# A fp32 transformer on one core: filter tiles and norm of the convolution mixer moved beside its attention, and a turned attention with values stationary in column tiles

## The reference

```python
def even_mixer(h, w_in, w_out, conv_w, conv_b, ln_g, ln_b, q_g, k_g, sinks):
    proj = h @ w_in
    a_val, a_gate, q, k, v = jnp.split(proj, cuts, axis=-1)
    u = a_val * jax.nn.sigmoid(a_gate)
    u = lax.conv_general_dilated(u, ...) + conv_b          # 31 taps, 512 channels
    u = jax.nn.silu(layer_norm(u, ln_g, ln_b))
    ...
    o, _, _ = banded_attention(q, k, v, SWA_WINDOW - 1, sinks)
    return jnp.concatenate([u, o.reshape(b, s, -1)], axis=-1) @ w_out

def causal_block_attention(q, k, v, scale):                # mla; dsa has the same with a mask from its index
    ...
        s = jnp.einsum('bqhd,bkhd->bhqk', qb, k).astype(jnp.float32) * scale
        s = jnp.where(key_pos[None, :] <= qpos[:, None], s, NEG)
        p = jax.nn.softmax(s, axis=-1).astype(v.dtype)
        return jnp.einsum('bhqk,bkhd->bqhd', p, v)
```

## Time and profile before

| | |
|---|---|
| median of three runs | 1776.69 us |
| the profiled execution | 1778.19 us |
| its span | 1776.4 us |
| mean granted TensorE clock | 0.997 |
| PE busy | 1757.5 us (99%), 9850 records |
| PEld busy | 1493.8 us (84%) |
| DVE busy | 1238.5 us (70%) |
| ACT busy | 934.9 us (53%) |
| POOL busy | 30.5 us (2%) |
| DMA | 312.06 MB, mean 176 GB/s |

### The profile page before, as it was taken

The page is one execution under the profiler, slowest core; times in us unless marked ns, Lnnn a source line. Parts: engine busy times, 40 slices in busy tenths (PEclk is TensorE's granted clock), DMA queues, the critical chain, the costliest instruction groups (busy, mean ns, idle before and its releaser), DMA issues.

```text
span 1776.4 us, 25138 instructions
## 1 busy us (share of the span) xinstructions
PE 1757.5 (99%) x9850; PEld 1493.8 (84%) x9850; DVE 1238.5 (70%) x1861; ACT 934.9 (53%) x1304; POOL 30.5 (2%) x41
## 2 busy tenths in 40 slices
PE   9999999999999999999999999999999999999998
PEld 8888878888888888888888788888888878888887
DVE  7776645876577657677656967777756778668774
ACT  6554545554455546555545545455544644555553
POOL 0000100000000001000000000000000000000000
PEclk9999999999999999999999999999999999999999
DMA  8656643666666656366656644556665554466663
GB/s 273 196 179 202 180 138 119 190 178 208 178 195 184 195 172 189 108 199 187 194 180 176 181 131 131 178 179 189 191 193 171 145 166 131 148 192 189 188 194 109
DMA packets 231294, 312.06 MB, mean 176 GB/s; under 512 B 23614, under 2 KB 179934, under 8 KB 231178
## 3 DMA queue, kind: packets, MB, share of 16 engines
q1 hardware_dynamic: 231014, 310.16, 57.7%
q10 hardware_dynamic: 164, 0.30, 0.0%
HBM read 308.71 MB, written 1.64 MB: 175 GB/s over the span
## 4 chain that ended last, share of the span: by engine, by line
PE 94%; DVE 4%; ACT 1%; issue 1%; DMA 0%; SPq 0%; POOL 0%; POOLq 0%; ACTq 0%
PE ps L657 26%; PE ps L606 16%; PE ps L608 16%; PE ps L607 16%; PE ps L659 13%; DVE wlo L1733 1%; PE ps L618 1%; PE ps L839 1%; PE ps L865 1%; PE ps L852 1%; PE ps L807 1%; ACT whi L1249 0%; DVE m_scr L1742 0%; PE ps L1151 0%; PE ps L902 0%
## 5 line engine op out<-in xcount | busy, mean ns | idle before, releaser
L1733 DVE TENSOR_TENSOR wlo<-staging,whi 128x1024 fp32r<-128x1024 f32 (+1 forms) x580 | 692.7, 1211 | 345.4 <-ACT whi L1249 344.9
L1249 ACT ACTIVATE whi<-staging 128x1024 fp32r<-128x1024 f32 (+1 forms) x580 | 606.5, 1050 | 489.8 <-PE ps L608 306.5
L657 PE MATMUL ps<-hT,whi 128*128 128x512 f32 x1984 | 623.6, 396 | 0.3 <-DVE wlo L1733 0.3
L659 PEld LDWEIGHTS ps<-hT,wlo 128*128 128x128 f32 x1984 | 372.7, 188 | 88.1
L659 PE MATMUL ps<-hT,wlo 128*128 128x256 f32 x1984 | 390.0, 278 | 0.0
L657 PEld LDWEIGHTS ps<-hT,whi 128*128 128x128 f32 x1984 | 302.1, 189 | 0.6 <-DVE wlo L1733 0.5
L606 PE MATMUL ps<-whi,fh 128*128 128x512 f32 x504 | 196.1, 389 | 0.0
L607 PE MATMUL ps<-wlo,fh 128*128 128x512 f32 x504 | 196.1, 389 | 0.0
L608 PE MATMUL ps<-whi,fl 128*128 128x512 f32 x504 | 196.1, 389 | 0.0
L606 PE MATMUL ps<-whi,hT 128*128 128x512 f32 (+3 forms) x464 | 184.2, 397 | 0.0
L608 PE MATMUL ps<-whi,hT 128*128 128x512 f32 (+3 forms) x464 | 177.4, 382 | 0.0
(11 more groups left out here) (345 smaller groups left out, 1829.9 us busy)
## 6 DMA issues: line engine op xcount, KB each, us to landing
staging<-in_w_in SPq DMA_DIRECT2D x92, 512.0 KB, 3.6
staging<-in_ffn_w_gate SPq DMA_DIRECT2D x84, 512.0 KB, 4.5
staging<-in_ffn_w_up SPq DMA_DIRECT2D x84, 512.0 KB, 4.5
staging<-in_ffn_w_down SPq DMA_DIRECT2D x84, 512.0 KB, 4.1
staging<-in_w_ffn_gate SPq DMA_DIRECT2D x44, 512.0 KB, 4.3
staging<-in_w_ffn_up SPq DMA_DIRECT2D x44, 512.0 KB, 4.6
staging<-in_w_ffn_down SPq DMA_DIRECT2D x44, 512.0 KB, 4.1
staging<-in_od_w_in SPq DMA_DIRECT2D x16, 512.0 KB, 3.7
```

Of the source, the lines that this page charges most:

```text
L657: e.matmul(o, wh[:, kk, j * 128:j * 128 + 128], hT[:, k, :], start=k == 0, stop=False)
L659: m = e.matmul(o[:, 0:256], wl[:, kk, j * 128:j * 128 + 128], hTh[:, k, :], start=False, stop=k == KD - 1)
L1249: e.activation(high(u)[:, 0:n], stage[u % NS][:, 0:n], ACT.Copy).then_inc(*K.inc("hi", ("hi", u)))
L1733: e.tensor_tensor(low_of(u)[:, 0:n], stage[u % NS][:, 0:n], high(u)[:, 0:n].bitcast(F32), ALU.subtract).then_inc(*K.inc("lo", ("lo", u)))
```

## The change

Two parts. In the even mixer the second half of the filter (`conv(2)`) becomes a generator of its own that starts in round 19 and stands behind `swa` in a round; it was a part of `products`, ahead of `swa`. The norm's mean moves from round 21 to 22, its variance from 23 to 25, and its broadcast from 25 to 27. The multiplication by the norm, Silu, and the high and low parts are made in two halves, and each row of the output product waits for its own half. The output product's `down` starts in round 23 as before.

In the four-branch mixers both attentions become `attend_turned`. Groups go by head pair: tile 0 and tile 1 of heads 0-1, then of heads 2-3. The probabilities are normalised before they are transposed: DVE takes the reciprocals of a group's sums (128x2) and ACT multiplies, two "light" copies. In the values matmuls v is stationary (128x64, in column tiles at output partitions 0 and 64) and the transposed probabilities move (128 columns), so that the output is already turned. The output scaling, the four transposes of outputs per attention and their wide copies go; ACT takes the high part (256 columns per head pair) from PSUM and DVE the low part a turn later.

```diff
@@ tensor program
+            def attend_turned(a):
+                groups = [(t, h0) for h0 in range(0, H, 2) for t in range(2)]
+                for turn in range(H + 3):
+                    sums = [turn - 3] if 0 <= turn - 3 < H else []
+                    for i in sums:
+                        t, h0 = groups[i]
+                        if t == 0:
+                            ops[h0] = room((P + " o", h0))
+                        e.wait_ge(*K.at(P + " pt", i))
+                        for kt in range(t + 1):
+                            for j in range(2):
+                                o = (j * (t + 1) + kt) * 128
+                                w = e.matmul(ops[h0][64 * j:64 * j + 64, 128 * t:128 * t + 128], a.vN(kt, h0 + j),
+                                             a.pt[i % 2][:, o:o + 128], start=kt == 0, stop=kt == t)
...
+                        e.wait_ge(*K.at(P + " light", i))
...
-                weave([(1, products()), (21, layer_norm()), (7, swa()), (23, down(g, m.rows))])
+                weave([(1, products()), (7, swa()), (19, conv(2)), (22, layer_norm()), (23, down(g, m.rows))])
...
-                    yield from attend(m.dat)
-                    yield
-                    transposed(P + "dsa", N(0, 256), 2)
+                    yield from attend_turned(m.dat)
@@ scalar program, in a turn after the exponentials
+                    if 0 <= turn - 3 < H and groups[turn - 3][0]:
+                        k = groups[turn - 3][1] // 2
+                        hi, _, at = a.dst
+                        e.wait_ge(*K.at(P + " pv", turn - 3))
+                        e.activation(hi[:, at + k, :], bk(P + " o", 2 * k)[:, 0:256], ACT.Copy).then_inc(
+                            *K.inc("oT", (P + " oT hi", k)))
+                    if 0 <= turn - 1 < H:
...
+                        e.wait_ge(*K.at(P + " one by", i))
+                        for j in range(2):
+                            e.activation(a.sm[i % 3][:, j, 0:nk], a.sm[i % 3][:, j, 0:nk], ACT.Copy,
+                                         scale=a.mx[:, 3, c0 + j:c0 + j + 1]).then_inc(
+                                *K.inc("light", *([(P + " light", i)] if j else [])))
@@ vector program
+                for turn in range(H + 3):
+                    if 0 <= turn - 4 and groups[turn - 4][0]:
+                        low(turn - 4)
+                    if 0 <= turn - 1 < H:
...
+                        e.wait_ge(*K.at(P + " ex", i))
+                        e.reciprocal(r, l).then_inc(*K.inc("att_sum", (P + " one by", i)))
+                    if turn < H:
...
+                            e.tensor_tensor_reduce(out=a.sm[i % 3][:, j, 0:nk], in0=ps[j][:, 0:nk],
+                                                   in1=a.mask(t), scale=scale(t, h0 + j),
...
-                weave([(1, products()), (18, conv()), (21, layer_norm()), (7, swa()), (23, down(g, m.rows, 1.0))],
+                weave([(1, products()), (18, conv()), (7, swa()), (22, layer_norm()), (23, down(g, m.rows, 1.0))],
```

More of the change, by code:

```diff
@@ L452, in __init__ @@
                              for k in range(4)]
-                self.rows += [(self.mh[:, k, :], self.ml[:, k, :], ("ev ml",)) for k in range(4)]
+                self.rows += [(self.mh[:, k, :], self.ml[:, k, :], ("ev ml", k // 2)) for k in range(4)]
         class Odd:
@@ L892, in products, with conv @@
                             done("ev u", j0 + j)
+                    yield from conv(0)
+                def conv(j0):
+                    ps = room(("ev tap", j0))
                     e.wait_ge(*K.at("ev w4"))
[L894 to L906, removed]
-                                yield
-                        done("ev tap", j0)
+                    for n in range(2 * STEPS):
+                        j, k = j0 + n // STEPS, n % STEPS
+                        if k == 0:
+                            e.wait_ge(*K.at("ev u4", j))
+                        c = 256 * (n // STEPS)
+                        for q in range(GROUPS):
+                            w = e.matmul(ps[32 * q:32 * q + 32, c:c + 256], m.w4[:, q, j, k, :],
+                                         m.u4[:, j, q, 4 * k:4 * k + S], start=k == 0, stop=k == STEPS - 1)
+                        if n + 1 == 2 * STEPS:
+                            w.then_inc(*K.inc("tap_mm", ("ev tap mm", j0)))
+                            done("ev tap", j0)
+                        if n + 1 in (6, 11, 16):
+                            yield
                 def swa():
@@ L1452, in swa @@
                     transposed("swa", 4, m.mh[:, 4:8, :])
-                weave([(1, products()), (6, swa()), (23, down(m.rows)), (21, layer_norm())], catch_up)
+                weave([(1, products()), (6, swa()), (22, layer_norm()), (23, down(m.rows))], catch_up)
             def odd(m):
@@ L1680, in mla @@
                     yield
[L1681 to L1683 removed]
+                    yield from attend_turned(m.mat)
                 def highs():
@@ L2390, in dsa @@
                     e.wait_ge(*K.now("dsa"))
-                    yield from attend(m.dat)
-                    yield
-                    transposed(P + "dsa", 2, m.bh[:, 4:6, :], m.bl[:, 4:6, :], (P, "branch", 2))
+                    yield from attend_turned(m.dat)
                 def gla():
@@ L2568, in mla @@
                         yield
-                    yield from attend(m.mat)
-                    yield
-                    transposed(P + "mla", 2, m.bh[:, 0:2, :], m.bl[:, 0:2, :], (P, "branch", 0))
+                    yield from attend_turned(m.mat)
                 weave([(1, gates()), (30, short_conv()), (1, dsa()), (5, gla()), (27, mla()), (TURN[0], turn()),
```

143 lines of the change are left out of this document (116 added, 27 removed).

## The result

Twenty runs of the changed kernel took 1782.85 us in the median (1778.08 to 1785.83), twenty of the kernel before, on the same chips, 1776.18 (1773.92 to 1780.03). The ratio on record is 1.0027, with a 95% interval of 1.0021 to 1.0034 (the two medians alone give 1.0038). The change made the kernel slower, by more than the forecast's bound of 0.2%, where no measurable change was forecast (1775.4). The time is above the stated range (1770.8 to 1780.0), and close to the rival B (1781.4), to which I had given 0.11.

The account below looks back on a forecast made before the run. TensorE bounds the kernel, busy 1757.5 of 1776.4 us. From 1778.19, less 2.2 (even mixer's order) and 3.0 (its clock), plus 2.4 (four-branch mixers), came 1775.4 us, range 1770.8 to 1780.0: no measurable change.

Parts of the forecast that it names:

- rival B: Four-branch mixers: the clock falls behind PE's 2.5 us idle, price 3.0 in each block, 1781.4 us; chance 0.11.
- even mixer, order and clock: Even mixer: 2.2 us gained by reordering PE's work and 3.0 by the clock no longer falling.
- wait (a): dsa, level matmuls: DVE's last score reduction starts late behind a reciprocal, PE's wait 1.1 to 2.5 us, +1.4 per block.
- wait (b): dsa, later level matmuls: PE waits for the outputs' PSUM bank until DVE's low part has read it, +1.4 per block.
- work of two attentions: Four-branch mixers, PE work: output transposes removed and values matmuls changed, 0.8 us less per attention.
- clock in the mixers: Four-branch mixers: no fall of the granted clock counted in the sum, 0 us; a fall was left to rival B.
- 1.86 idle was harmless before taps: Argument against rival B: PE's 1.86 us idle ahead of the even mixer's taps brought no fall of the clock.
- 0.75 us of new waits: Even mixer: some 0.3 us at the second turn's transposes and some 0.45 at the mean, taken as 0.75 together.
- "nothing" for the norm in two halves: Even mixer, output products: PE does not wait for normalised rows in either order, so no gain, unless late (about 0.5).
- the 0.63 taken: Four-branch mixers, values matmuls in column tiles: a block of eight was to take 0.63 us, against 0.84 before.
- the rule: Values matmuls: "Mode switching requires drain", quoted against the change; no size given, as taps run without a visible gap.
- upper bound of +7: Four-branch mixers, both blocks together: +7 us at the worst of new waits and PE work, where +2.4 was taken.

Follow-up runs that it names:

- both edits: Changed kernel with DVE's reciprocal behind the next scores' reduction and its low part of the outputs a turn earlier, ahead of the weight remainder: 1771.46 us, 0.9965 of before.
- norm late: Kernel before with only the norm a round later (mean in round 22, variance in 25, broadcast in 27), taps unmoved: 1781.14 us, 1.0017 of before.
- probes: Even mixer's part of the change, old attention, plus unused DVE additions ahead of dsa's last score reduction: three gave 1.0021, one 0.9999 of the kernel before.
- even part alone: Kernel before with only the even mixer's part of the change, attention of the four-branch mixers as before: 1773.58 us, 0.9971 of before.
- order of the tiles: Kernel with both edits, but the values matmuls run all of one head, then all of the other: 1771.56 us, 0.9967 of the kernel before.

## Why the prediction was wrong

The two profiled executions, term by term:

| term of the sum | forecast | measured |
|---|---|---|
| even mixer, order and clock | -5.2 | -4.95 |
| wait (a), per block | +1.4 | +1.37 |
| wait (b), per block | +1.4 | +1.74 and +1.59 |
| work of two attentions, per block | -1.6 | -1.24 and -1.00 (the mixers with both edits, where neither new wait stands) |
| clock in the mixers, both | 0 | about +6 |

**The step that failed** is "Against it: 1.86 idle was harmless before taps", with which I put the mixers' clock at nothing in the sum and gave rival B 0.11. I had the mechanism and its place, the wait of 2.5 us at L1201. In its place the runs showed 6.2 us of the clock in the profiled execution, as worked out below. One execution had one wait of 1.86 us with no fall behind it and one of 1.17 with a fall, and I read from these that it depends on what PE runs afterwards. The kernel with the turned attention alone showed a fall at the very same taps, with 2.27 us of idle time, so the taps are no protection; and one execution without a fall could not show that a wait is harmless, as the kernel with the norm late had none there with 2.73. The probes showed one behind 1.67 and 2.86 us with the old attention, in all of their profiled blocks, while the kernel with both edits, where PE idles 1.1 us at that place, has a mean clock of 0.998 to 1.000 in all five runs. What stood in the profile for it was plain: the change took the idle time at the level matmuls from 1.1 to 2.5 us in each block, where the longest of a mixer had been 1.3, and the one fall of its clock stood behind a wait of only 1.17. What stays open is why the place matters: around dsa's last scores the clock fell in 11 of 12 profiled blocks with an idle time of 1.6 us or more, while of nine idle times of 1.7 us or more at the start of the program and in the even mixer only three had a fall. So my thought that it also depends on what PE runs around the wait is not refuted; what failed is to read safety from one wait.

By the stages, the two mixers are 10.0 us longer, less 1.9 a block for waits and work, 6.2 us; the three windows above hold 3.42 + 6.33 + 3.41 us of PE's work at half speed, 6.6 by the other way. That this is near rival B's 6.0 is partly luck: the windows cost 1.7 us in the first block and 4.9 in the second, not 3.0 in each, and four of the twenty runs kept a mean of 0.998. 1783.48 - 6.2 = 1777.3 us. Of the 1.9 that are left against 1775.4, the work is 1.0, the second wait 0.5, the even mixer 0.25.

**The even mixer** went as forecast: both waits gone, the fall gone, 0.75 us of new waits taken and 0.7 found (265.83 against the pure work's 265.12, counted from the scores at 248.41, which in the trace of before began at 248.28; the larger gaps are those ahead of the turn at 251.11 and of the mean at 264.22, 0.5 in all). But "nothing" for the norm in two halves was wrong. In place of that, the norm a round later would have cost 2.5 us of waiting at the first normalised rows, and the halves pay for it. The two errors cancelled, so this term came out right by luck: the step was priced with the whole change made, and PE waited only 0.2 us there. Beside 24 runs of before of which 20 had a mean of 0.997 or less, the part was worth 5.2 us; beside runs in which the clock falls less often it should be worth less, which was not measured.

**Both new waits** came at the place worked out, the first to the tenth and the second within 0.35 us, (a) by the reciprocal, which stands ahead of the reduction and waits for ACT (3.83 us idle, until 1018.17), (b) by the low part of the outputs behind a weight remainder that waits for ACT. Each went when only the order on DVE was changed.

**The work** gave less. The block of transposes was worth about 0.45, as taken. The values' blocks of eight went from 0.84 to 0.59 us, better than the 0.63 taken. What I left out is the change of shape around them. PE before, around the last block of values in mla, and then the same block after:

```profile
1112.12 0.40 PE L608 MATMUL ps<-whi,hT 128*128 128x512 f32 x1
1112.36 1.00 PE L839 MATMUL ps<-m_scr 128*128 128x64 f32 x8
1113.17 0.47 PE L606 MATMUL ps<-whi,hT 128*128 128x512 f32 x1
1113.48 0.39 PE L607 MATMUL ps<-wlo,hT 128*128 128x512 f32 x1
```

```profile
1111.55 0.39 PE L609 MATMUL ps<-whi,hT 128*128 128x512 f32 x1
1111.87 0.66 PE L888 MATMUL ps<-m_scr 128*64 128x128 f32 x8
1112.45 0.50 PE L607 MATMUL ps<-whi,hT 128*128 128x512 f32 x1
1112.80 0.40 PE L608 MATMUL ps<-wlo,hT 128*128 128x512 f32 x1
```

The last product ahead of the block takes 0.32 us start to start instead of 0.24, and the first one behind it 0.35 instead of 0.31; where four transposes follow instead, they take 0.41 (1108.53 to 1108.94) instead of 0.37 (1109.15 to 1109.52). That is 0.12 us per block, four blocks to an attention, and eats most of what two blocks of eight gain (0.5). It is what the Trainium skill says, page "TensorEngine Tiling (Array Packing)", section Key Properties: a change of the tiling mode drains the engine. The trace agrees, with 0.08 us in and 0.04 out. I had quoted the rule and set it aside because the taps run without a gap; but the taps are all of one mode inside a block, and the switch stands at its edges. Nor was it so that no row had it: four transposes took 0.36 us ahead of a full-array product (1041.96 to 1042.32) and 0.53 ahead of the level matmuls in 32-row tiles (1030.53 to 1031.06). The same page's section Theoretical Speedup gives up to 2x for 64 columns; the block of eight went down to 0.7 of itself with twice the moving columns, the values of a whole attention by about 0.1 us.

**Two sums** of the forecast were off, with nothing resting on them: 0.36 less for the values of an attention makes 1.4 for four, not 1.3; and the upper bound of +7 for both blocks does not follow from its parts, as 2 x (2.2 + 2.4) - 3.2 is 6.0 with the work as taken, and 9.0 with the column tiles not overlapping.

## What to carry to other kernels

A new wait of 1 to 2 us of TensorE can cost more than itself: look at the granted clock behind each idle time in several executions, and put its loss in the sum with a chance (here 1.2 us of waiting cost some 3 more). One wait without a fall behind it does not show that waits of its length are harmless. When a reciprocal or a copy is added to an in-order engine, put it behind the instruction for which TensorE waits, and not ahead of it: two reorderings on DVE turned +0.27% into -0.35%. A matmul in another tiling pays at both edges of its block, so short blocks of it gain little.

## What the runs showed of the hardware that was not expected

Outside the last microseconds of the program every fall of the clock lasted 3.41 or 6.83 us, and four of the thirteen profiles have none (the even part alone, both edits, the order of the tiles, the norm late). A fall does not come in every execution: with the same wait of 2.43 us in both blocks, one execution had 6.83 us at 0.50 in the first and none in the second. With dsa's longest idle time at 1.1 us it fell there in none of the profiles, and with 1.6 us or more in 11 of 12 profiled blocks. But the length alone does not order the cases. Two waits of 1.17 us ahead of the even mixer's output transposes and two of 0.99 at the index scores had a fall behind them; 26 waits of 1.3 us at L1251 and its like, one of 1.74 that began 5 us behind the end of an earlier fall, and one of 2.73 ahead of the taps had none.

How often the kernel before loses it differs between sets of runs on one chip: its mean clock was 0.997 in 19 of 24 runs of one set and in 13 of 27 of another, which had 1774.1 to 1774.5 us at 0.999 and 1779.8 to 1781.4 at 0.996. So a part of what a change seems to be worth depends on the runs beside which it is measured, and the mean clock of each run has to stand beside its time.
